# Neighbourhood attention: the context units spread in pairs over the four latent blocks, their outputs in the bank of the output transposes

## The chip, the cores and the metric

The kernel runs on one core of a Trainium2 chip. The metric is the device time of one launch in microseconds (us). TensorE is called PE below (PEld is its weight load), VectorE DVE, ScalarE ACT, GpSimd POOL and SyncE SP.

## The reference

One inference step of a two-layer trunk for 128 context tokens and 512 latent tokens with the same weights. Each layer has a mixer of three branches (differential attention, a state-space branch, neighbourhood attention) and a mixture of experts. Only the neighbourhood attention is touched. It has 8 heads of 64. Context tokens attend to all 128 context tokens:

```python
def block_attention(q, k, v):          # context: 8 heads, 128 queries, 128 keys
    ...
    s = jnp.einsum("bhqd,bhkd->bhqk", qi, k).astype(jnp.float32) * scale
    return jnp.einsum("bhqk,bhkd->bhqd", jax.nn.softmax(s, axis=-1).astype(v.dtype), v)

def neighbourhood_attention(q, k, v, kc, vc, rpb):   # latents, on a grid of 8 x 64
    ...                                # per block of 16 columns: 128 queries
        s_w = jnp.einsum("bhjqd,bhjkd->bhjqk", qi, kg).astype(jnp.float32) * scale + bi[None]
        s_x = jnp.einsum("bhjqd,bhcd->bhjqc", qi, kc).astype(jnp.float32) * scale
        pr = jax.nn.softmax(jnp.concatenate([s_w, s_x], axis=-1), axis=-1).astype(v.dtype)
        return (jnp.einsum("bhjqk,bhjkd->bhjqd", pr[..., :nk_blk], vg)
                + jnp.einsum("bhjqc,bhcd->bhjqd", pr[..., nk_blk:], vc))
```

A latent block has 256 window keys with a relative bias and a mask, and 128 cached context keys. The bias is added before the softmax.

## The kernel before

The program is written by hand for each engine, and semaphores alone order the engines against each other. `stage_na` runs once in each layer. It first projects v, q and k and gathers the values of each window into `vg`. Then comes the loop that the change touches.

**Units.** One unit is one block of 128 queries and one head. `units` lists them: block 0 (the context, 8 units), then blocks 1 to 4 of latents (8 each), 40 in all. Two units that follow each other are a pair, whose scores are computed together.

**What a unit does.** PE writes the scores into a bank of its own (banks 0 to 3 in turn; L1821 for the context, L1826 and L1829 for latents). DVE finds the maximum: for a context unit with one reduce from PSUM (L1950); for a latent unit it adds mask and raw bias (L1955), adds that to the scores and takes the maximum while it writes `pr` (L1960), and negates it (L1964). ACT takes the exponential into `pr` with the row sum (L1918 context, L1923 latent). PE transposes `pr` (`turn`, L1837: one transpose for the context, three for latents), ACT copies the result to `pT` (`evacuate`, L1910), and PE multiplies by the values into bank 6 (`values`, L1848 or L1853 and L1854). `pr` and `pT` have two buffers.

**The order on PE.** For pair g with the units 2g and 2g+1: scores of pair g+1, turn(2g), values(2g-1), turn(2g+1), values(2g). The order on ACT is exp(u), evacuate(u-1); on DVE it is maxima(u) in turn.

**The end of a block.** All eight heads of a block fill bank 6. After maxima of the second unit of the next block DVE waits for the last values of the block, forms reciprocals (L1969) and multiplies bank 6 into `o` (`take`, L1974). The first values of the next block wait for that, since they write the same bank. Two units on, PE transposes `o` in four pieces into bank 7 (`output`, L1863), and after the sixth unit's maxima DVE copies bank 7 in four pieces (L1988) to `oT` (`spill`), from which the next stage reads (PE L1269). After the last unit `take`, `output` and `spill` follow one another with nothing beside them.

**SP** issues the loads of the raw bias (L1734), four buffers ahead: load n waits for the mask addition of latent unit n-4.

## Time and profile before

| what | value |
|---|---|
| median of 3 runs | 2922.89 us (2920.81 to 2929.72) |
| the profiled execution | 2923.79 us, its span 2922.0 us |
| PE busy | 86% of the span |
| DVE, ACT, POOL busy | 32%, 20%, 13% |
| the loop over units, layer 0 | from 843.9 to 914.2 us of the span |
| the loop over units, layer 1 | from 2245.4 to 2313.8 us |

The two loops are 139 us of 2922. PE's granted clock is a share of 2.4 GHz: 1.00 is 2.4 GHz and 0.50 is 1.2 GHz.

### The profile page before, as it was taken

The page shows a single profiled execution, that of the slowest core. Times are in us where ns is not written, and L with a number is a line of the kernel's source. Part 1 is how long each engine was busy: PE and PEld are TensorE (multiplying, and loading weights), DVE is VectorE, ACT ScalarE, POOL GpSimd, SP SyncE. Part 2 cuts the span into 40 slices and gives each one's busy share as a digit, 9 for nine tenths or more (in the row PEclk, how much of TensorE's full clock was granted, in tenths as well). Part 3 has the DMA queues.
Part 4 walks back from the last instruction along what each step waited for, and adds up shares of the span by engine and source line. Part 5 has one row for each costly group of instructions (what it writes and reads, how often), then busy time and mean ns, then how long its engine had stood idle before and what let it go on. Part 6 is the DMA issues. An engine that isn't in the chain of part 4 may idle for free. (4 is left out here: it accounts for less than half of the span.)

```text
span 2922.0 us, 36075 instructions
## 1 busy us (share of the span) xinstructions
PE 2506.1 (86%) x13898; PEld 1488.6 (51%) x13898; DVE 944.7 (32%) x1843; ACT 598.7 (20%) x1392; POOL 366.8 (13%) x390
## 2 busy tenths in 40 slices
PE   5999999779999898868749998987999998988775
PEld 2445644556467546434325565545646764654442
DVE  1414311552026235111325242236301633522115
ACT  2221101430033021111142111024001401211111
POOL 0005100020002000222100250001200210022220
PEclk7999999899989998989969999989999999889997
DMA  8440053102631121788432102110033203075764
GB/s 311 145 149 33 29 201 134 37 1 80 201 99 32 63 94 70 281 334 312 170 129 96 37 29 75 36 58 1 29 129 96 43 29 119 29 269 226 279 235 180
DMA packets 170108, 357.95 MB, mean 123 GB/s; under 512 B 35076, under 2 KB 56684, under 8 KB 169972
## 3 DMA queue, kind: packets, MB, share of 16 engines
q1 hardware_dynamic: 129812, 267.70, 25.8%
q10 hardware_dynamic: 22176, 46.37, 4.6%
q0 software_dynamic: 17984, 42.01, 3.9%
q8 instruction: 92, 1.51, 0.2%
q14 instruction: 44, 0.36, 0.0%
HBM read 331.60 MB, written 47.48 MB: 130 GB/s over the span
## 5 line engine op out<-in xcount | busy, mean ns | idle before, releaser
L226 PE MATMUL ps<-hT,ring 128*128 128x512 f32 x896 | 413.4, 616 | 13.6 <-PEq L2822 12.4
L2297 PE MATMUL ps<-ring,mixT 128*32 128x256 f32 x2880 | 234.3, 407 | 73.4 <-issue 73.4
L226 PEld LDWEIGHTS ps<-hT,ring 128*128 128x128 f32 x896 | 172.8, 198 | 231.1 <-issue 230.8
L2297 PEld LDWEIGHTS ps<-ring,mixT 128*32 128x32 f32 x2880 | 124.5, 118 | 191.6 <-issue 129.1
L235 PE MATMUL ps<-ring,hT 128*128 128x512 f32 x480 | 211.8, 599 | 8.4 <-PEq L1182 7.4
L1220 POOL TENSOR_TENSOR mix_S<-ring 128x512 f32<-128x512 f32 x16 | 25.3, 1579 | 1160.7 <-POOLq L1357 607.4
L2181 PE MATMUL ps<-ring,mixT 128*128 128x512 f32 x320 | 143.9, 610 | 21.0 <-PEq L2822 21.0
L235 PEld LDWEIGHTS ps<-ring,hT 128*128 128x128 f32 x480 | 91.2, 192 | 122.1 <-issue 120.0
L1269 PE MATMUL ps<-late,ring 128*128 128x320 f32 x512 | 142.7, 436 | 5.6 <-PEq L1698 2.5
L2315 PE MATMUL ps<-ring,ex_hidT 128*32 128x512 f32 x800 | 117.1, 603 | 22.0 <-ACT ex_hidT L2404 22.0
L228 PEld LDWEIGHTS ps<-hT,ring 128*128 128x128 f32 x896 | 108.8, 192 | 26.8 <-issue 26.8
L1269 PEld LDWEIGHTS ps<-late,ring 128*128 128x128 f32 x512 | 96.9, 191 | 49.0 <-issue 9.5
L649 PE MATMUL ps<-hT,ring 128*128 128x512 f32 x256 | 112.8, 593 | 0.4 <-ACT ssm_dec L906 0.4
L2181 PEld LDWEIGHTS ps<-ring,mixT 128*128 128x128 f32 x320 | 62.1, 196 | 97.8 <-issue 97.8
L228 PE MATMUL ps<-hT,ring 128*128 128x128 f32 x896 | 109.1, 275 | 0.0
L1234 PE MATMUL ps<-mix_T,mix_S 128*128 128x320 f32 x384 | 106.0, 432 | 0.0
L2592 DVE TENSOR_TENSOR ex_hid<-ps,ex_silu 128x128 f32<-128x128 f32 x60 | 17.5, 291 | 271.4 <-ACT ex_silu L2399 271.4
L1234 PEld LDWEIGHTS ps<-mix_T,mix_S 128*128 128x128 f32 x384 | 73.0, 190 | 30.4
L2284 PE MATMUL ps<-base,mixT 128*128 128x128 f32 x496 | 68.6, 282 | 14.6 <-DMA mixT<-h_rows,ex_index 14.6
L649 PEld LDWEIGHTS ps<-hT,ring 128*128 128x128 f32 x256 | 48.4, 191 | 58.9 <-issue 58.8
L2609 DVE COPY out_gpost<-ps 128x512 f32<-128x512 f32 x60 | 41.5, 692 | 108.9 <-PE ps L2315 108.9
L2284 PEld LDWEIGHTS ps<-base,mixT 128*128 128x128 f32 x496 | 53.9, 142 | 40.1 <-issue 25.8
(439 smaller groups left out, 3904.2 us busy)
## 6 DMA issues: line engine op xcount, KB each, us to landing
ring<-in_w_in SPq DMA_DIRECT2D x18, 2048.0 KB, 9.1
ring<-in_w_gate SPq DMA_DIRECT2D x12, 2048.0 KB, 10.6
ring<-in_w_e_down SPq DMA_DIRECT2D x48, 512.0 KB, 11.9
ring<-in_w_e_gate SPq DMA_DIRECT2D x40, 512.0 KB, 7.7
ring<-in_w_e_up SPq DMA_DIRECT2D x40, 512.0 KB, 9.2
co_yg<-y_rows SPq DMA_DIRECT2D x40, 512.0 KB, 6.8
mixT<-in_w_ada ACTq DMA_DIRECT2D x8, 2048.0 KB, 8.7
da_ada_w<-in_w_ada ACTq DMA_DIRECT2D x8, 2048.0 KB, 8.9
```

The costliest lines, as they stand in the source:

```text
L226: pe.matmul(lat, wide[:, k, c], hT[:, k, CTX:TOK], start=(k == 0), stop=(k == kt_n - 1))
L228: last = pe.matmul(ctx, wide[:, k, c], hT[:, k, 0:CTX], start=(k == 0), stop=(k == kt_n - 1))
L235: last = pe.matmul(out, cx.hT[:, k, tok(t)], wide[:, k, :], start=(k == 0), stop=(k == KT - 1))
L649: ins = pe.matmul(ps[:, 6, :], wide[:, k, (m % 4) * P:(m % 4 + 1) * P], cx.hT[:, k, CTX:TOK], start=(k == 0), stop=(k == KT - 1))
L1220: pool.tensor_tensor(s1, a21, a22, ALU.add).then_inc(name("sums"), 1)
L1234: ins = pe.matmul(ps[:, bank(q, i), 0:HALF], left[:, k, :], right[:, k, :], start=(k == 0), stop=(k == KH - 1))
L1269: ins = pe.matmul(ps[:, BR + 2 * c + x, 0:HALF], wb[:, k, (2 * q + c) * P:(2 * q + c + 1) * P], cx.oT[:, k, half], start=(k == 0), stop=(k ...
L2181: ins = pe.matmul(ps[:, 2 * (t % 2) + n, :], cx.mixT[:, k, tok(t)], wide[n][:, k, :], start=(k == 0), stop=(k == KT - 1))
L2284: ins = pe.transpose(ps[:, k // 4, (k % 4) * P:(k % 4 + 1) * P], xg[:, b, k * P:(k + 1) * P], cx.ident)
L2297: ins = pe.matmul(ps[rows, 2 + b, 0:2 * P].rearrange("p (g f) -> p g f", g=2), xT[:, b, k, rows], ew[:, :, k, :], start=(k == 0), stop=(k ...
L2315: ins = pe.matmul(ps[rows, 4 + 2 * b + h, :], hidT[:, b, rows], slots[LANES * (s % 2) + c][1][:, h * SEC:(h + 1) * SEC], start=True, stop= ...
L2609: dve.tensor_copy(y[:, b, SEC:D], ps[:, 5 + 2 * b, :]).then_inc(sem("y_high"), 1)
```

## The change

The units get another order. Each latent block has four of its units, then two context units, then its other four: ten units in each of four rounds (`UPB`). The context's values go to the first 128 columns of bank 7, no longer to bank 6, and a small `take_ctx` on DVE brings each pair to `oc` (the free quarter of `vlo`), so that bank 6 holds latents alone. The values of the next context pair wait until bank 7 was spilled. The outputs come in the order of blocks 1, 2, 3, context, 4 (`taken`); that of the context stands just ahead of the last unit's values. Semaphore counts follow (`latents_to`). The diff, with the declarations of shapes left out:

```diff
--- before.py
+++ after.py
@@ -1694,7 +1694,17 @@
     KW = TOK + PAST
     ALLK = NKEY + PAST
 
-    units = [(b, h) for b in range(1 + NBLK) for h in range(NA_H)]
+    units = []
+    for b in range(1, 1 + NBLK):
+        units += [(b, h) for h in range(4)] + [(0, 2 * b - 2), (0, 2 * b - 1)] + [(b, h) for h in range(4, NA_H)]
+    UPB = NA_H + 2
+    latent = [unit for unit in units if unit[0]]
+    taken = list(range(1, NBLK)) + [0, NBLK]
+
+    def latents_to(u):
+
+        return sum(b > 0 for b, h in units[:u])
+
     with ExitStack() as st:
         def sb(name, shape):
             return st.enter_context(nc.sbuf_tensor(f"{name}_{L}", shape, F32))
...
@@ -1811,7 +1822,7 @@
                     if units[2 * g - 4][0] == 0:
                         pe.wait_ge(sem("na_exp"), 2 * g - 2)
                     else:
-                        pe.wait_ge(sem("na_s_read"), 2 * g - 2 - NA_H)
+                        pe.wait_ge(sem("na_s_read"), latents_to(2 * g - 2))
                 c = h // 2
                 q = [qT[64 * x:64 * x + 64, c, tok(b)] for x in range(2)]
                 k = [kT[64 * x:64 * x + 64, c, :] for x in range(2)]
@@ -1840,11 +1851,14 @@
             def values(u):
                 b, h = units[u]
                 pe.wait_ge(sem("na_pT_out"), u + 1)
-                if h == 0 and b >= 1:
-                    pe.wait_ge(sem("na_o_out"), b)
+                if h == 0 and b >= 2:
+                    pe.wait_ge(sem("na_o_out"), b - 1)
                 out = ps[:, 6, h * 64:(h + 1) * 64]
                 c = slice(h * 64, (h + 1) * 64)
                 if b == 0:
+                    if h >= 2 and h % 2 == 0:
+                        pe.wait_ge(sem("ona_out"), h // 2)
+                    out = ps[:, 7, (h % 2) * 64:(h % 2 + 1) * 64]
                     ins = pe.matmul(out, pT[:, u % 2, 0, :], v0[:, 0, c], start=True, stop=True)
                 else:
                     if b == 1 and h == 0:
@@ -1854,13 +1868,17 @@
                     ins = pe.matmul(out, pT[:, u % 2, 2, :], v0[:, 1, c], start=False, stop=True)
                 ins.then_inc(sem("na_o_mm"), 1)
 
-            def output(b):
-
-                pe.wait_ge(sem("na_o_out"), b + 1)
+            def output(n):
+
+                b = taken[n]
                 if b:
-                    pe.wait_ge(sem("ona_out"), b)
+                    pe.wait_ge(sem("na_o_out"), b)
+                pe.wait_ge(sem("na_c_out"), min(n + 1, NBLK))
+                if n:
+                    pe.wait_ge(sem("ona_out"), n)
+                src = o[:, (b - 1) % 2, :] if b else oc
                 for c in range(4):
-                    ins = pe.transpose(ps[:, 7, c * P:(c + 1) * P], o[:, b % 2, c * P:(c + 1) * P], cx.ident)
+                    ins = pe.transpose(ps[:, 7, c * P:(c + 1) * P], src[:, c * P:(c + 1) * P], cx.ident)
                 ins.then_inc(sem("ona_turned"), 1)
 
             ada.taken(pe, 4)
@@ -1872,8 +1890,9 @@
                 turn(u)
                 if u:
                     values(u - 1)
-                if u % NA_H == 2 and u > NA_H:
-                    output(u // NA_H - 1)
+                if u % UPB == 2 and u > UPB:
+                    output(u // UPB - 1)
+            output(NBLK - 1)
             values(len(units) - 1)
             output(NBLK)
 
@@ -1916,10 +1935,10 @@
                     act.wait_ge(sem("na_turned"), u - 1)
                 if b == 0:
                     act.activation(pr[:, u % 2, 0:CTX], ps[:, u % 4, 0:CTX], ACT.Exp, bias=nmx[:, u % 4:u % 4 + 1],
-                                   accum_out=sm[:, b % 2, h:h + 1]).then_inc(sem("na_exp"), 1)
+                                   accum_out=sm[:, 2, h:h + 1]).then_inc(sem("na_exp"), 1)
                 else:
-                    if h == 0 and b >= 2:
-                        act.wait_ge(sem("na_o_out"), b - 1)
+                    if h == 0 and b >= 3:
+                        act.wait_ge(sem("na_o_out"), b - 2)
                     act.activation(pr[:, u % 2, :], pr[:, u % 2, :], ACT.Exp, bias=nmx[:, u % 4:u % 4 + 1],
                                    accum_out=sm[:, b % 2, h:h + 1]).then_inc(sem("na_exp"), 1)
                 if u:
@@ -1950,7 +1969,7 @@
                     dve.tensor_reduce(nmx[:, u % 4:u % 4 + 1], ps[:, u % 4, 0:CTX], AX.X, ALU.max,
                                       negate=True).then_inc(sem("na_max"), 1)
                     return
-                n = u - NA_H
+                n = latents_to(u)
                 dve.wait_ge(sem(f"na_raw{n % 4}"), 16 * (n // 4 + 1))
                 dve.tensor_tensor(bias[:, u % 2, 0:NKEY], raw[:, n % 4, :], mask[:, b - 1, :], ALU.add).then_inc(
                     sem("na_bias_ready"), 1)
@@ -1964,20 +1983,34 @@
                 dve.tensor_scalar(nmx[:, u % 4:u % 4 + 1], mx[:, u % 4:u % 4 + 1], -1.0, None, ALU.mult).then_inc(
                     sem("na_max"), 1)
 
-            def take(b):
-
+            def take(b, u):
+
+                dve.wait_ge(sem("na_o_mm"), u)
+                dve.wait_ge(sem("na_exp"), u)
                 step(dve, dve.reciprocal(rc[:, b % 2, :], sm[:, b % 2, :]))
-                if b >= 2:
-                    dve.wait_ge(sem("ona_turned"), b - 1)
+                if b >= 3:
+                    dve.wait_ge(sem("ona_turned"), b - 2)
                 else:
                     dve.wait_ge(sem("na_v_dumped"), 64)
-                dve.tensor_tensor(o[:, b % 2, :].rearrange("p (h d) -> p h d", h=NA_H),
+                dve.tensor_tensor(o[:, (b - 1) % 2, :].rearrange("p (h d) -> p h d", h=NA_H),
                                   ps[:, 6, :].rearrange("p (h d) -> p h d", h=NA_H),
                                   spread(rc[:, b % 2, :], 2, NA_HD), ALU.mult).then_inc(sem("na_o_out"), 1)
 
-            def spill(b):
-
-                dve.wait_ge(sem("ona_turned"), b + 1)
+            def take_ctx(n, u):
+
+                pair = slice(2 * n, 2 * n + 2)
+                dve.wait_ge(sem("na_o_mm"), u)
+                dve.wait_ge(sem("na_exp"), u)
+                step(dve, dve.reciprocal(rc[:, 2, pair], sm[:, 2, pair]))
+                dve.wait_ge(sem("na_v_dumped"), 64)
+                dve.tensor_tensor(oc[:, n * P:(n + 1) * P].rearrange("p (x d) -> p x d", x=2),
+                                  ps[:, 7, 0:P].rearrange("p (x d) -> p x d", x=2), spread(rc[:, 2, pair], 2, NA_HD),
+                                  ALU.mult).then_inc(sem("na_c_out"), 1)
+
+            def spill(n):
+
+                b = taken[n]
+                dve.wait_ge(sem("ona_turned"), n + 1)
                 src = ps[:, 7, :].rearrange("p (c q) -> p c q", c=4)
                 for c in range(4):
                     if b == 0:
@@ -1990,15 +2023,14 @@
 
             for u, (b, h) in enumerate(units):
                 maxima(u)
-                if u >= NA_H and h == 1:
-                    dve.wait_ge(sem("na_o_mm"), b * NA_H)
-                    dve.wait_ge(sem("na_exp"), b * NA_H)
-                    take(b - 1)
-                if u >= NA_H and h == 5:
-                    spill(b - 1)
-            dve.wait_ge(sem("na_o_mm"), len(units))
-            dve.wait_ge(sem("na_exp"), len(units))
-            take(NBLK)
+                if u % UPB == 1 and u > UPB:
+                    take(u // UPB, UPB * (u // UPB))
+                if u % UPB == 5 and u > UPB:
+                    spill(u // UPB - 1)
+                if u % UPB == 8:
+                    take_ctx(u // UPB, u - 2)
+            spill(NBLK - 1)
+            take(NBLK, len(units))
             spill(NBLK)
 
 
```

The first place is PE's start of the loop in layer 0. The rows of before: context scores (L1821, two pairs), then transposes (L1837) and values (L1848) of one context unit each.

```order
L1821 MATMUL ps<-na_kT_0,na_qT_0 128x128 x4
L1837 MATMUL ps<-base,na_pr_0 128x128 x2
L1848 MATMUL ps<-na_v0_0,na_pT_0 128x64
L1821 MATMUL ps<-na_kT_0,na_qT_0 128x128 x2
L1837 MATMUL ps<-base,na_pr_0 128x128
L1848 MATMUL ps<-na_v0_0,na_pT_0 128x64
L1837 MATMUL ps<-base,na_pr_0 128x128
L1848 MATMUL ps<-na_v0_0,na_pT_0 128x64
```

The rows of the change at the same place, where L1837 and L1840 are the scores of a latent pair, L1848 the transposes, L1867 and L1868 the values of a latent unit, and L1832 the scores of a context pair:

```order
L1837 MATMUL ps<-na_kT_0,na_qT_0 128x256 x2
L1840 MATMUL ps<-na_kT_0,na_qT_0 128x128 x2
L1837 MATMUL ps<-na_kT_0,na_qT_0 128x256 x2
L1840 MATMUL ps<-na_kT_0,na_qT_0 128x128 x2
L1848 MATMUL ps<-base,na_pr_0 128x128 x6
L1867 MATMUL ps<-na_vg_0,na_pT_0 128x64 x2
L1868 MATMUL ps<-na_v0_0,na_pT_0 128x64
L1832 MATMUL ps<-na_kT_0,na_qT_0 128x128 x2
L1848 MATMUL ps<-base,na_pr_0 128x128 x3
L1867 MATMUL ps<-na_vg_0,na_pT_0 128x64 x2
L1868 MATMUL ps<-na_v0_0,na_pT_0 128x64
```

The first two score pairs are now latent ones, of two matmuls of 256 and two of 128 columns each, and the first context scores come after the values of one latent unit.

The second place is PE's rows around the first context pair (units 4 and 5) in the changed kernel; L1862 is the values of a context unit.

```order
L1837 MATMUL ps<-na_kT_0,na_qT_0 128x256 x2
L1840 MATMUL ps<-na_kT_0,na_qT_0 128x128 x2
L1848 MATMUL ps<-base,na_pr_0 128x128
L1867 MATMUL ps<-na_vg_0,na_pT_0 128x64 x2
L1868 MATMUL ps<-na_v0_0,na_pT_0 128x64
L1848 MATMUL ps<-base,na_pr_0 128x128
L1862 MATMUL ps<-na_v0_0,na_pT_0 128x64
L1837 MATMUL ps<-na_kT_0,na_qT_0 128x256 x2
L1840 MATMUL ps<-na_kT_0,na_qT_0 128x128 x2
L1848 MATMUL ps<-base,na_pr_0 128x128 x3
L1862 MATMUL ps<-na_v0_0,na_pT_0 128x64
```

Each of the context unit's transposes and values now stands between the transposes and values of latent units; before, all eight were ahead of the first of these.

The third place is PE's end of the loop. Before (L1863 is the output's transposes):

```order
L1837 MATMUL ps<-base,na_pr_0 128x128 x3
L1853 MATMUL ps<-na_vg_0,na_pT_0 128x64 x2
L1854 MATMUL ps<-na_v0_0,na_pT_0 128x64
L1853 MATMUL ps<-na_vg_0,na_pT_0 128x64 x2
L1854 MATMUL ps<-na_v0_0,na_pT_0 128x64
L1863 MATMUL ps<-base,na_vlo_0 128x128 x4
```

And in the changed kernel (L1881 the output's transposes):

```order
L1848 MATMUL ps<-base,na_pr_0 128x128 x3
L1867 MATMUL ps<-na_vg_0,na_pT_0 128x64 x2
L1868 MATMUL ps<-na_v0_0,na_pT_0 128x64
L1881 MATMUL ps<-base,na_vlo_0 128x128 x4
L1867 MATMUL ps<-na_vg_0,na_pT_0 128x64 x2
L1868 MATMUL ps<-na_v0_0,na_pT_0 128x64
L1881 MATMUL ps<-base,na_vlo_0 128x128 x4
```

The transposes of the context's output moved from the first latent block to this place, ahead of the last unit's values.

## Rows read from the trace of the kernel before

**Rows 1.** The page's first part, PE: busy, share, instructions; PEld and others follow.

```profile
PE 2506.1 (86%) x13898; PEld 1488.6 (51%) x13898; DVE 944.7 (32%) x1843; ACT 598.7 (20%) x1392; POOL 366.8 (13%) x390
```

**Rows 2.** Busy by stretch: length, PE, PEld, DVE, ACT, POOL, PEclk, DMA share, GB/s.

```profile
843.90:914.20 70.30, 64.40 (x477) 55.95 (x477) 45.37 (x167) 41.04 (x120) 0.03 (x1) 0.86 0.30 66
2245.40:2313.80 68.40, 62.22 (x477) 54.23 (x477) 45.39 (x167) 41.03 (x120) 0.04 (x1) 0.90 0.37 89
844.00:864.00 20.00, 19.05 (x89) 15.33 (x90) 8.67 (x31) 9.62 (x37) 0.00 (x0) 0.50 0.31 73
865.00:914.00 49.00, 44.27 (x381) 39.51 (x379) 36.46 (x135) 31.08 (x83) 0.00 (x0) 1.00 0.29 63
2245.40:2249.80 4.40, 3.56 (x26) 2.45 (x26) 1.37 (x6) 3.07 (x16) 0.00 (x0) 1.00 1.01 364
2250.00:2263.50 13.50, 13.07 (x62) 10.91 (x62) 7.21 (x25) 6.30 (x20) 0.00 (x0) 0.50 0.42 91
```

**Rows 3.** Timeline, PE, latent pairs at 2.4 GHz: start, busy, engine, line.

```profile
865.17 0.70 PE L1826 MATMUL ps<-na_kT,na_qT 64*128 64x256 f32 x4
...
866.02 0.55 PE L1837 MATMUL ps<-base,na_pr 128*128 128x128 f32 x3
...
868.07 0.70 PE L1826 MATMUL ps<-na_kT,na_qT 64*128 64x256 f32 x4
...
884.24 0.70 PE L1826 MATMUL ps<-na_kT,na_qT 64*128 64x256 f32 x4
...
888.15 0.70 PE L1826 MATMUL ps<-na_kT,na_qT 64*128 64x256 f32 x4
...
889.14 0.55 PE L1837 MATMUL ps<-base,na_pr 128*128 128x128 f32 x3
...
891.72 0.70 PE L1826 MATMUL ps<-na_kT,na_qT 64*128 64x256 f32 x4
```

**Rows 4.** Timeline, DVE, at 2.4 GHz, the last two after the end of a block.

```profile
869.02 0.43 DVE L1955 TENSOR_TENSOR na_bias<-na_raw,na_mask 128x256 f32<-128x256 f32 x1 [0.39 <-PE ps L1829]
...
887.14 0.42 DVE L1955 TENSOR_TENSOR na_bias<-na_raw,na_mask 128x256 f32<-128x256 f32 x1
...
888.30 0.42 DVE L1955 TENSOR_TENSOR na_bias<-na_raw,na_mask 128x256 f32<-128x256 f32 x1
```

**Rows 5.** Timeline, PE, a context pair at 2.4 GHz, layer 1.

```profile
2247.90 0.49 PE L1821 MATMUL ps<-na_kT,na_qT 64*128 64x128 f32 x4
2248.32 0.33 PE L1837 MATMUL ps<-base,na_pr 128*128 128x128 f32 x1
...
2249.38 0.49 PE L1821 MATMUL ps<-na_kT,na_qT 64*128 64x128 f32 x4
```

**Rows 6.** Timeline, PE and PEld, the start of the loop in layer 0.

```profile
843.93 1.23 PE L1821 MATMUL ps<-na_kT,na_qT 64*128 64x128 f32 x8 [4.54 <-ACT na_kT L1902]
...
851.50 1.23 PE L1826 MATMUL ps<-na_kT,na_qT 64*128 64x256 f32 x4
...
859.86 1.23 PE L1826 MATMUL ps<-na_kT,na_qT 64*128 64x256 f32 x4
...
861.44 0.90 PE L1837 MATMUL ps<-base,na_pr 128*128 128x128 f32 x3
...
863.09 0.87 PEld L1863 LDWEIGHTS ps<-base,na_vlo 128*128 128x128 f32 x4
```

**Rows 7.** Timeline, all engines, the end of the loop in layer 0.

```profile
904.99 0.70 PE L1826 MATMUL ps<-na_kT,na_qT 64*128 64x256 f32 x4
...
910.38 0.66 PE L1853 MATMUL ps<-na_vg,na_pT 128*128 128x64 f32 x4
...
911.30 0.20 DVE L1969 RECIPROCAL na_rc<-na_sm 128x8 f32<-128x8 f32 x1 [2.84 <-PE ps L1854]
...
912.98 0.88 DVE L1988 COPY late<-ps 128x128 f32<-128x128 f32 x4 [0.75 <-PE ps L1863]
...
914.19 6.16 PE L1269 MATMUL ps<-late,ring 128*128 128x320 f32 x22 [1.24 <-PEq L1698]
```

More of the change, by code:

```diff
@@ L1711, in stage_na @@
         o = vlo[:, 2:4, :]
+        oc = vlo[:, 1, :]
         stage = sb("na_stage", [P, NA_H, NA_HD])
@@ L1714, in stage_na @@
         nmx = sb("na_nmx", [P, 4])
-        sm = sb("na_sm", [P, 2, NA_H])
-        rc = sb("na_rc", [P, 2, NA_H])
+        sm = sb("na_sm", [P, 3, NA_H])
+        rc = sb("na_rc", [P, 3, NA_H])
         if L + 1 < DEPTH:
@@ L1729, in load_raw @@
             def load_raw(n):
-                b, h = units[NA_H + n]
+                b, h = latent[n]
                 at = h * RPB_ROW + RPB_FRONT + col0(b - 1) - QB_C * (b - 1)
```

## Prediction

> **What bounds the kernel now.** I read the page first, then the stretches, then the timeline of the loop. The page shows TensorE (PE) busy for 86% of the span and no other engine above 32% [rows 1]. The two loops over units take 70.3 and 68.4 us [rows 2], 138.7 of 2922, so 0.3% of the kernel (8.8 us, about what a measurement can tell from no change) is 6% of what the change touches.
>
> Inside the loop at 2.4 GHz PE is busy 44.3 of 49.0 us, DVE 36.5 and ACT 31.1 [rows 2]. A plain latent pair takes 2.90 us from scores to scores (865.17 to 868.07), of which the scores are 0.85 (to 866.02) [rows 3], and the two units 1.03 each. DVE needs 1.16 per unit (887.14 to 888.30) [rows 4], 2.32 per pair, so it isn't the limit: PE is. Where a block ends PE loses time: the pair whose second values wait for `take` lasts 3.91 (884.24 to 888.15), 1.01 more, and the next, which has the four transposes of `output` and an exponential that comes late, lasts 3.57 (to 891.72), 0.67 more [rows 3]. So a block takes 2 x 2.90 + 3.91 + 3.57 = 13.28 us.
>
> The other limit is PE's clock. It stood at 1.2 GHz from 844 to 864 in layer 0, and in layer 1 it was at 2.4 GHz to 2249.8 and at 1.2 from 2250 to 2263.5 [rows 2]. At 1.2 GHz the scores of a latent pair take 1.58 (859.86 to 861.44) and a unit's transposes and values 1.65 (861.44 to 863.09) [rows 6]: 4.88 a pair, so each microsecond of dense latent work at 1.2 GHz costs 1 - 2.90/4.88 = 0.41 us.
>
> **What the change removes and adds, all at 2.4 GHz first.** The matmuls, exponentials and maxima of all units are as many as before. I lay the new order out in slots, one for each pair, and add them up.
>
> The start. Before, the loop began with light context pairs; the first latent scores came 7.57 us in (843.93 to 851.50) [rows 6]. Now latents fill the pipeline. A bias addition starts 0.95 after its scores (868.07, 869.02) [rows 3, 4], and the transposes 2.00 after the bias addition (887.14, 889.14) [rows 3, 4]. So unit 0 is transposed at 2.95, unit 1 (1.16 later on DVE) at 4.1, and after ACT's copy the values of unit 0 end at about 5.1. Two pairs' scores (1.7) lie inside. First slot: 5.1; it can't be under 4.1 (unit 1), nor over the 6.3 that it takes at 1.2 GHz.
>
> A context pair among latents. At 2.4 GHz its scores take 0.42 (2247.90 to 2248.32) and the rest of its 1.48 (to 2249.38) is 1.06 for two units, with a wait in it [rows 5]. The slot of the context pair holds the next latent pair's scores (0.85), the values of the latent unit before (the larger part of 1.03, I take 0.62) and two context transposes and one context values (0.70 of that 1.06): 2.17. The slot ahead of it has context scores in place of latent ones: 0.43 less work, of which I keep 0.34, so 2.56. In blocks 2 to 4 that gain is zero, because there PE waits for the exponential anyway until 0.99 after the scores began (888.15, 889.14) [rows 3]: 3.57 stays. The slot behind it has 2.40 us of PE work, but PE has come there too early. DVE starts the bias of unit 6 at 0.95 of the context slot and that of unit 7 1.16 later, at 2.11; its transposes can start 2.00 after that, at 4.11; PE would be there at 2.17 + 1.30 = 3.47. It waits 0.64, and some 0.1 more for ACT's copy: 3.13, or 0.23 more than a plain pair. So each context pair costs 2.06 in block 1 and 2.40 in the others. **Bounds of this term:** below, nothing waits and it costs its PE work alone, 1.29 (0.42, and 1.06 less the wait of about 0.2); above, as much as a latent pair, 2.90. I take the chain since each of its links is a row.
>
> DVE gains four `take_ctx` per loop: a reciprocal and a 128x128 product, between nothing and 0.20 + 0.88/4 (the 128x8 reciprocal and one of the four copies of 128x128 [rows 7]), 0.42. In the slot behind the context pair DVE has fewer than 2.9 us of work in the 3.13, and four times in a loop the 0.42 lies there; if that cover were gone it would be 1.7 a loop. `spill` leaves its place between two latent maxima and lies where DVE has only two short context maxima; the wait of the next context values for it ends before PE comes there (about 7.5 against 9.3 us from the start of the block's `take` slot), so I cost it at nothing.
>
> Removed: one `take` stall (1.01) and one `output` slot (0.67), since only three block ends lie inside the loop now. They do not come back in full: the context's `output` and `spill` stand at the end. Before, DVE's last reciprocal started 0.92 after the last values (910.38, 911.30) [rows 7]. Now the context's four transposes come ahead of these values, and its copies (0.88 like those at 912.98 [rows 7]) keep DVE to about 911.83: 0.53 later.
>
> The sum of a loop at 2.4 GHz: block 1 is 5.1 + 2.56 + 2.17 + 3.13 + 2.90 = 15.86; blocks 2 and 3 are 3.91 + 3.57 + 2.17 + 3.13 + 2.90 = 15.68 each; block 4 is 3.91 + 3.57 + 2.17 = 9.65, then the last two pairs with the drain, 9.20 before (904.99 to 914.19 [rows 7]), plus 0.23 and 0.53. Together 66.8 us.
>
> **The clock.** Before, PE was busy 19.05 of 20.00 us at 1.2 GHz in layer 0 [rows 2], and the clock still rose only some 4 us after the third latent pair's scores (859.86 [rows 6], 864), that is in the first stretch in which latent transposes and values ran without a stop; the context units and the stall for the first `take` lay before. In the changed order the first such stretch is units 1 and 2, about 6 to 10 us into the loop. I take the rise there. Layer 0 then starts at 1.2 GHz (the 4.54 us idle before the loop [rows 6] stays), the fill takes 6.3 in place of 5.1, and 3.7 us of dense work cost 1.3 more: 66.8 + 2.5 = 69.3, against 70.3 before, 1.0 less. In layer 1 the fill leaves PE idle more than the context units did, so the clock falls as before some 4.4 us in; with some 3.5 us at 1.2 GHz it costs 1.4 (0.41 of each): 68.2 against 68.3 or 68.4, 0.1 less.
>
> The Trainium skill (TensorE: Matmul & The Clock Gate, Part 1) says that sustained matmul activity is what releases the slow clock. The 19.05 busy us at 1.2 GHz do not agree with that rule taken alone [rows 2]. By that rule the changed loop, dense with latents from its first microsecond, would be at 2.4 GHz in layer 0 before the fill is over, and the sum of that loop would be about 68.
>
> Sum: 1.0 + 0.1 = 1.1 us less. The profiled execution of before took 2923.79, 0.9 more than the median of 2922.89; less 1.1 that is 2922.7, and 2922 on the scale of the median.
>
> **The rivals.**
> The clock rises late (this one ends on the slower side). The stretch of units 1 and 2 is cut by the context pair right behind it, whose units are as light as those that ran at 1.2 GHz before. If it isn't enough, slots 2 to 4 run at 1.2 GHz too: context slot 3.9, the next 4.4, the fourth 4.88, together 13.2 against 8.2 at 2.4 GHz: 5.0 more per layer, so +4 in one layer and +9 with both, 2926 to 2932. For it: latents now run in the slow time that cheap context units used to fill, and these lost less there. It decides from the point that both layers are late.
>
> The context pairs cost only their PE work. Then each costs 1.29, not 2.06 to 2.40: 8.5 us less over both loops, 2913. For it speaks that DVE has 36.5 of 49 us [rows 2]; against it the chain from bias to transposes, 2.00 us in rows, that a short slot can't cover.
>
> The clock hardly falls. If layer 1 stays at 2.4 GHz and layer 0 rises within the fill, the loops take 66.8 and 68 (66.8 and the 1.2 by which the fill is longer): 3.9 less than before, 2919. Against it: with context units PE was busy 3.56 of 4.40 us [rows 2], and the clock fell.
>
> The raw bias comes late in layer 1. Load 4 is now issued some 7 us sooner, into DMA engines whose share was 1.01 in the first 4.4 us of that loop [rows 2] with a weight section and two stores. It is needed 9 us in. If it misses by what remains of that queue I estimate 2 us: 2924.
>
> **How the numbers follow.** My forecast has 0.50 (2922, by itself 2918 to 2926). Late clock: one layer 0.15, both 0.12. Context hidden 0.06. Clock hardly falls 0.10. Raw bias late 0.05, other 0.02. More than 0.3% slower is above 2931.7: late in both layers and the rest, 0.14. More than 0.3% faster is below 2914.1: context hidden, 0.06. Same: 0.80. The range is 2915 to 2933: it takes in the late clock in both layers and leaves out the hidden context.
>
> **What would show it.** Scores to scores in the changed trace: 2.2 for the context slot, 3.1 for the slot behind, with PE waiting for ACT's exponential of the block's fifth or sixth latent head; 3.91 still at three block ends, no longer at the first; the granted clock back at 1.00 about 854 us in layer 0 and 8 us into the loop in layer 1; the four context copies on DVE, some 0.5 us of them past the last values, ahead of the last reciprocal. The prediction is wrong if the clock stays at 0.50 past the second context pair, if PE waits for DVE's `spill` ahead of context values, or if a bias addition waits for a DMA.

## The result and the profile after

| | before | changed |
|---|---|---|
| median of 8 runs each | 2929.34 us (2916.45 to 2938.97) | 2942.20 us (2936.72 to 2949.04) |
| ratio, with its 95% interval | 1 | 1.0047 (1.0025 to 1.007) |
| the profiled execution, its span | 2923.79, 2922.0 us | 2936.91, 2935.1 us |
| loop over units, layer 0 | 70.3 us | 78.7 us |
| loop over units, layer 1 | 68.4 us | 71.1 us |

The changed kernel is 0.47% slower, where 0.04% faster was forecast, and its 2942.20 lies outside the range of 2915 to 2933. The kernel before took 6.4 us more here than the 2922.89 from which the forecast started; on that base 1.0047 would be 2936.6, outside the range as well. All ratios leave out three later executions (two of the kernel before, one with fills) of 5117 to 5254 us. Of the 13.1 us between the two spans, 11.1 lie in the two loops. The stages outside, whose code is the same, make up the other 2.0 (2785.3 us against 2783.3).

The page, its first part, changed kernel, against [rows 1]:

```profile
PE 2508.4 (85%) x13898; PEld 1489.8 (51%) x13898; DVE 946.5 (32%) x1855; ACT 597.5 (20%) x1392; POOL 366.5 (12%) x390
```

PE has as many instructions as before, and DVE twelve more. Nothing there tells of 13 us. The stretches do (length, PE, PEld, DVE, ACT, POOL, PEclk, DMA share, GB/s): first the two loops, then what lies inside them by granted clock, against [rows 2].

```profile
844.60:923.30 78.70, 70.12 (x477) 61.24 (x477) 46.35 (x173) 40.57 (x120) 0.04 (x1) 0.80 0.27 60
2258.60:2329.70 71.10, 61.03 (x476) 53.40 (x477) 46.35 (x172) 40.50 (x120) 0.00 (x0) 0.93 0.35 86
844.60:862.50 17.90, 16.82 (x82) 14.41 (x83) 7.62 (x28) 7.32 (x23) 0.00 (x0) 0.50 0.39 98
...
873.00:876.00 3.00, 3.00 (x16) 2.80 (x16) 0.88 (x4) 1.25 (x6) 0.00 (x0) 0.50 0.16 50
...
890.00:900.00 10.00, 10.00 (x51) 8.95 (x51) 4.36 (x17) 3.95 (x14) 0.00 (x0) 0.50 0.20 41
2258.60:2296.00 37.40, 31.81 (x270) 27.66 (x271) 26.62 (x98) 23.49 (x69) 0.00 (x0) 1.00 0.50 129
2296.50:2306.00 9.50, 9.50 (x48) 8.47 (x48) 3.88 (x14) 3.76 (x13) 0.00 (x0) 0.50 0.19 42
```

What to see: before, the clock rose once in each loop and stayed up to its end. Now it rises at 862.7, 18 us into layer 0, and then falls twice inside the latent blocks (about 872.7 to 876.2 and 889.8 to 900.1), and once in layer 1 (2296.1 to 2306.4). Read to 0.1 us, that is about 31.6 and 10.2 us at 1.2 GHz in the two loops, against 20.2 and 13.7 before. The forecast had about 10 and 3.5.

Layer 1 shows the new order at 2.4 GHz undisturbed for 37 us. Timeline of PE there (start, busy, engine, line; in brackets the idle time ahead and what ended it). L1837 is the scores of a latent pair, L1832 those of a context pair, L1848 transposes, L1867 values:

```profile
2258.60 0.70 PE L1837 MATMUL ps<-na_kT,na_qT 64*128 64x256 f32 x4 [0.83 <-ACT na_kT L1921]
...
2263.92 0.49 PE L1832 MATMUL ps<-na_kT,na_qT 64*128 64x128 f32 x4
...
2266.39 0.70 PE L1837 MATMUL ps<-na_kT,na_qT 64*128 64x256 f32 x4
...
2268.41 0.70 PE L1837 MATMUL ps<-na_kT,na_qT 64*128 64x256 f32 x4
...
2270.57 0.55 PE L1848 MATMUL ps<-base,na_pr 128*128 128x128 f32 x3 [0.45 <-ACT na_pr L1942]
...
2271.76 0.70 PE L1837 MATMUL ps<-na_kT,na_qT 64*128 64x256 f32 x4
...
2274.66 0.70 PE L1837 MATMUL ps<-na_kT,na_qT 64*128 64x256 f32 x4
...
2277.79 0.63 PE L1867 MATMUL ps<-na_vg,na_pT 128*128 128x64 f32 x4 [0.78 <-DVE na_vlo L1995]
...
2278.57 0.49 PE L1832 MATMUL ps<-na_kT,na_qT 64*128 64x128 f32 x4
2279.56 0.55 PE L1848 MATMUL ps<-base,na_pr 128*128 128x128 f32 x3 [0.50 <-ACT na_pr L1942]
...
2282.13 0.70 PE L1837 MATMUL ps<-na_kT,na_qT 64*128 64x256 f32 x4
...
2284.15 0.70 PE L1837 MATMUL ps<-na_kT,na_qT 64*128 64x256 f32 x4
...
2286.30 0.55 PE L1848 MATMUL ps<-base,na_pr 128*128 128x128 f32 x3 [0.49 <-ACT na_pr L1942]
...
2287.49 0.70 PE L1837 MATMUL ps<-na_kT,na_qT 64*128 64x256 f32 x4
...
2290.39 0.70 PE L1837 MATMUL ps<-na_kT,na_qT 64*128 64x256 f32 x4
```

From scores to scores, measured against forecast: fill 5.32 (5.1), context-score slot 2.47 (2.56), context slot 2.02 (2.17), the slot behind 3.35 (3.13), plain pair 2.90 (2.90). The next block: `take` 3.91 (3.91), `output` 3.56 (3.57), context 2.02 (2.17), behind 3.34 (3.13), plain 2.90. The first block is 16.06 against 15.86 and the second 15.73 against 15.68. So no slot is off by more than 0.22 us.

The same slots where the clock falls in the middle, layer 0, PE (L1881 is the transposes of `output`):

```profile
887.11 0.63 PE L1867 MATMUL ps<-na_vg,na_pT 128*128 128x64 f32 x4 [0.78 <-DVE na_vlo L1995]
...
887.89 0.49 PE L1832 MATMUL ps<-na_kT,na_qT 64*128 64x128 f32 x4
888.88 0.55 PE L1848 MATMUL ps<-base,na_pr 128*128 128x128 f32 x3 [0.50 <-ACT na_pr L1942]
...
890.02 1.06 PE L1881 MATMUL ps<-base,na_vlo 128*128 128x128 f32 x4
...
892.83 1.23 PE L1837 MATMUL ps<-na_kT,na_qT 64*128 64x256 f32 x4
...
896.53 1.23 PE L1837 MATMUL ps<-na_kT,na_qT 64*128 64x256 f32 x4
...
900.66 0.70 PE L1837 MATMUL ps<-na_kT,na_qT 64*128 64x256 f32 x4
```

The two waits (0.78 for `take`, 0.50 for an exponential) lie within 2.6 us, from 886.33 to 888.88. Behind them the `output` transposes take 1.06 in place of 0.61, and the slots 4.94, 3.70 and 4.13 in place of 3.56, 2.02 and 3.34. All three falls inside the blocks come at this point of a block, in its `output` slot.

In the old order the same place has one wait, not two. There the 0.78 for `take` stands as well, but the scores that follow are those of a latent pair; they last until 889.08 and the transposes start at 889.14 [rows 3], so the wait for the exponential is 0.06:

```profile
888.69 0.39 PE L1829 MATMUL ps<-na_kT,na_qT 64*128 64x128 f32 x4
```

The context scores are shorter, and leave 0.50 of it open.

### The profile page after: what moved, and what is told of

It reads as the page before. It is cut to its first block and busy times, and to the rows that moved or that the text cites. A ratio compares the mean times of both kernels' runs of the same rounds, so it can differ in the third digit from the quotient of the medians.

```text
span 2935.1 us, 36111 instructions
## 1 busy us (share of the span) xinstructions
PE 2508.4 (85%) x13898; PEld 1489.8 (51%) x13898; DVE 946.5 (32%) x1855; ACT 597.5 (20%) x1392; POOL 366.5 (12%) x390
## 5 line engine op out<-in xcount | busy, mean ns | idle before, releaser
L2329 PEld LDWEIGHTS ps<-ring,mixT 128*32 128x32 f32 x2880 | 124.6, 118 | 190.1 <-issue 127.7
L2316 PE MATMUL ps<-base,mixT 128*128 128x128 f32 x496 | 70.3, 286 | 16.2 <-DMA mixT<-h_rows,ex_index 16.0
L2316 PEld LDWEIGHTS ps<-base,mixT 128*128 128x128 f32 x496 | 55.2, 145 | 41.8 <-issue 27.3
```

The lines of the kernel that those rows point to most:

```text
L2316: ins = pe.transpose(ps[:, k // 4, (k % 4) * P:(k % 4 + 1) * P], xg[:, b, k * P:(k + 1) * P], cx.ident)
L2329: ins = pe.matmul(ps[rows, 2 + b, 0:2 * P].rearrange("p (g f) -> p g f", g=2), xT[:, b, k, rows], ew[:, :, k, :], start=(k == 0), stop=(k ...
```

## The experiments

My theory was that the falls come from the stretch between `take` and the end of the `output` slot, where three light places now stand together: the wait for `take`, the slot with context scores and its wait for an exponential, and the context slot. The rivals were that the new order is longer at any clock, that the low start is what costs, that the shared bank 7 costs something, and that the bias on DVE is the late link. Two remarks hold for all: single executions of one kernel differ by up to 1% here (the kernel before took 2915.80 to 2943.76 in 34 of them, and the same code outside the two loops took 2782.6 to 2796.2 us in the twelve traces), so that medians of 5 to 12 runs are compared with runs of the kernel before on the same chip; and matmuls called fills multiply values already in place into bank columns that nobody reads (those ahead of a loop into a bank that the scores overwrite), so that they change no result. Each run has one traced execution.

### The changed kernel again

No edit.

> The changed kernel once more, as a base for the others on the same chip. Both theories: 10 to 15 us over before. Theory C (clock): in each loop of the trace the granted clock falls to 0.50 again inside the blocks, right behind a take slot that is followed by a slot with context scores, and loop time is about 66.8 to 67.5 us plus 0.35 to 0.4 us for each microsecond at 0.50. Where the falls come may differ from one execution to the next. Theory D (dependencies alone): the loops take the same time whatever the clock does, and the extra lies in slots that are longer than before at the same clock.

Measured: 2945.96 us against 2927.69, 1.0063 (1.0043 to 1.0083). The loops took 78.50 and 74.64 us. Layer 0 again rose 18 us in, fell at 876.3, 28.0 us in, as far in as in the first trace (872.7 is 28.1 in), stayed down for 10 and fell once more at 910.4 for 3.4. Layer 1, which had not fallen at its start in the first trace, fell 5 us in here for 6.8, and again at 2320.5 for 10. All three falls inside blocks lie in `output` slots again. So a fall at a block's end recurs, while which blocks it hits differs from one execution to the next.

### Fills at the block ends

```diff
             def turn(u):
+                if u % UPB == 2 and u > UPB:
+                    pe.wait_ge(sem("na_pT_out"), u - 1)
+                    for _i in range(2):
+                        pe.matmul(ps[:, 4 + u % 2, 384:512], cx.ident, cx.hT[:, 0, 0:P], start=True, stop=True)
...
                 if h == 0 and b >= 2:
+                    for _i in range(3):
+                        pe.matmul(ps[:, 4 + u % 2, 384:512], cx.ident, cx.hT[:, 0, 0:P], start=True, stop=True)
```

> The changed kernel with matmuls of no use (results never read) where PE waits inside the blocks: three of 128x128 ahead of the wait for take, two ahead of the wait for the exponential one pair later, 0.24 us each at 2.4 GHz, in waits of 0.78 and 0.50 us. Theory C: more work for PE, yet the clock stays at 1.00 once it has risen, in both layers; the falls of 3.4, 10.3 and 10.2 us go, and the kernel is 7 to 10 us faster than the changed kernel. Theory D: the clock may stay up, but the time is the same or up to 2 us longer than that of the changed kernel, as each take slot stays at 3.91.

Measured: 2934.34 against 2927.69, 1.0028 (1.0009 to 1.0047), that is 11.6 us less than the changed kernel beside it (2945.96), with more for PE to do. Window from the rise to the end of the loop in layer 1:

```profile
2265.20:2322.80 57.60, 53.51 (x448) 47.06 (x446) 40.91 (x153) 35.29 (x104) 0.00 (x0) 1.00 0.27 56
```

After the low start each loop stayed at 2.4 GHz through all its block ends, for 57.6 us here and for 58 in layer 0. The loops took 71.52 and 70.33, 11.3 less than without fills. What follows: the falls inside the blocks hang on the waits at the block ends. By the medians the edit wins back 11.6 of the 18.3 us that the changed kernel lost on this chip. Not all of it need be those falls: in this trace the low start of layer 0 was 13.4 us long, not 18, though nothing was edited there.

### The context pair two units later

```diff
-        units += [(b, h) for h in range(4)] + [(0, 2 * b - 2), (0, 2 * b - 1)] + [(b, h) for h in range(4, NA_H)]
+        units += [(b, h) for h in range(6)] + [(0, 2 * b - 2), (0, 2 * b - 1)] + [(b, h) for h in range(6, NA_H)]
...
-                if u % UPB == 8:
-                    take_ctx(u // UPB, u - 2)
+                if u % UPB == 9:
+                    take_ctx(u // UPB, u - 1)
```

> The changed kernel with the context pair behind the sixth latent unit of each block, not the fourth, so that the slot with context scores is no longer the one with output's transposes. Theory C: PE's sparse slots stand apart, so the clock falls less often inside blocks: 5 to 10 us faster than the changed kernel. Theory D: the chain from bias to transposes is the same behind each context pair, so only the 0.34 us that the context scores save in a slot of their own comes back, three times a loop: about 2 us faster.

Measured: 2937.50 against 2927.69, 1.0038 (1.0022 to 1.0055), 8.5 us less than the changed kernel. The `output` slot now holds latent scores and is followed by a plain pair. Windows, layer 0, then layer 1:

```profile
855.00:908.50 53.50, 48.60 (x409) 42.45 (x408) 37.64 (x141) 34.72 (x107) 0.00 (x0) 1.00 0.27 59
2254.00:2270.50 16.50, 16.50 (x81) 14.62 (x81) 5.47 (x21) 7.02 (x23) 0.00 (x0) 0.50 0.39 92
2271.50:2318.50 47.00, 42.16 (x353) 36.81 (x353) 33.90 (x127) 30.31 (x91) 0.00 (x0) 1.00 0.27 57
```

Its PE rows at a block's end, layer 0:

```profile
866.13 0.63 PE L1867 MATMUL ps<-na_vg,na_pT 128*128 128x64 f32 x4 [0.65 <-DVE na_vlo L1995]
...
867.45 0.39 PE L1840 MATMUL ps<-na_kT,na_qT 64*128 64x128 f32 x4
867.90 0.55 PE L1848 MATMUL ps<-base,na_pr 128*128 128x128 f32 x3
```

No fall in the middle of a block is left. The loops were low at the start (in layer 0 down, up and down again in the first 10 us), and in the last 5 us of each; they took 69.66 and 75.05 us. The rows show why the block ends differ: the wait for `take` is still 0.65, but the latent scores run to 867.84 and the transposes start at 867.90, so the second wait is gone, as in the old order [rows 3], which stayed up too. So in these traces the `take` stall alone did not bring the clock down. Context scores in this place did, and they come with two things at once, less work for PE and a second wait of 0.50; which of them counts no run tells apart.

### The other bank alone, in the old order

```diff
-                if h == 0 and b >= 1:
+                if h == 0 and b >= 2:
                     pe.wait_ge(sem("na_o_out"), b)
-                out = ps[:, 6, h * 64:(h + 1) * 64]
+                out = ps[:, 6 if b else 7, h * 64:(h + 1) * 64]
```

(and the same bank in `take`).

> The order of before with one part of the change: the context's values go to bank 7, all eight heads, so that the first latent block's values need not wait for its take. Theory C and D alike: the first take stall goes (0.8 to 1.7 us a loop at 1.2 GHz), 2 to 3 us faster than before, within 0.3% of it. If the time rises by over 5 us, it is the bank, and not the order, that costs.

Measured: 2924.40 against 2927.69, 0.9994 (0.9978 to 1.0009), no difference. Its PE row at the first block end, layer 0:

```profile
858.56 0.55 PE L1837 MATMUL ps<-base,na_pr 128*128 128x128 f32 x3 [0.43 <-ACT na_pr L1923]
```

The wait for `take` is gone there, but the exponential is waited for. At 2.4 GHz the bank gains 0.13 us a loop, as the two experiments after this one show. So in the old order the bank costs nothing that can be measured. In the changed order bank 7 is also shared with the output transposes; there no context values (L1862) waited in either trace of the changed kernel.

### The old order with fills

```diff
+            for _i in range(4 if L == 0 else 1):
+                pe.matmul(ps[:, 3, :], cx.ident, cx.hT[:, 0, 0:512], start=True, stop=True)
             pe.wait_ge(sem("na_kc_out"), 1)
...
+                for _i in range(3 if u == 0 else 0):
+                    pe.matmul(ps[:, 4 + u % 2, 384:512], cx.ident, cx.hT[:, 0, 0:P], start=True, stop=True)
                 pe.wait_ge(sem("na_exp"), u + 1)
...
                 if h == 0 and b >= 1:
+                    for _i in range(3):
+                        pe.matmul(ps[:, 4 + u % 2, 384:512], cx.ident, cx.hT[:, 0, 0:P], start=True, stop=True)
                     pe.wait_ge(sem("na_o_out"), b)
```

(the wait for the exponential now stands behind that for `na_pT_out` and the fills).

> The order of before, with matmuls of no use (never read) where PE waits: four of 128x512 (layer 1: one) in the 4.5 us ahead of the loop, three of 128x128 ahead of the first exponential's wait and three ahead of each take's wait. It shows the old order at one clock. Theory C: the granted clock stays at 1.00 in most of both loops, each loop takes 64 to 65 us (70.3 and 68.3 before), and the kernel is 6 to 10 us faster than before. Theory D: the loops stay within 1 us of 70 and 68.

Measured: 2920.13 against 2926.41, 0.9974 (0.996 to 0.9989): faster than the kernel before, by 0.26%. Window of its loop in layer 0 (that of layer 1 is alike):

```profile
850.40:914.20 63.80, 59.66 (x506) 52.92 (x506) 45.35 (x166) 40.61 (x120) 0.00 (x0) 1.00 0.32 72
```

This is the number that my prediction lacked: the old order at 2.4 GHz from end to end takes 63.85 us a loop (63.87 and 63.83). The loops lost 10.9 us in the trace and the median 6.3. The interval of the ratio, 3.2 to 11.7 us, holds both, so nothing says that a part did not reach the end of the kernel.

### The same with the other bank

The two edits above together; with bank 7 the fills at block ends begin a block later.

```diff
-                if h == 0 and b >= 1:
+                if h == 0 and b >= 2:
+                    for _i in range(3):
+                        pe.matmul(ps[:, 4 + u % 2, 384:512], cx.ident, cx.hT[:, 0, 0:P], start=True, stop=True)
                     pe.wait_ge(sem("na_o_out"), b)
-                out = ps[:, 6, h * 64:(h + 1) * 64]
+                out = ps[:, 6 if b else 7, h * 64:(h + 1) * 64]
```

(and the same bank in `take`).

> The same fills, and the context's values in bank 7 for the order of before (no take stall for the first latent block). Theory C: loops of 63 to 64 us, 8 to 13 us faster than before in all. Theory D: only the first take stall goes, 2 to 3 us.

Measured: 2921.13 against 2926.41, 0.9974 (0.9956 to 0.9992). Loops of 63.74 and 63.71 us, 0.13 less each than with bank 6. In the run with this bank and no fills layer 1 took 63.58 us, at 2.4 GHz nearly throughout, so the fills themselves add next to nothing.

### The changed order with fills everywhere

The block-end fills of the second experiment, and those at the start:

```diff
+            for _i in range(4 if L == 0 else 1):
+                pe.matmul(ps[:, 3, :], cx.ident, cx.hT[:, 0, 0:512], start=True, stop=True)
             pe.wait_ge(sem("na_kc_out"), 1)
...
+                for _i in range({0: 4, 1: 2}.get(u, 2 if u % UPB == 2 and u > UPB else 0)):
+                    pe.matmul(ps[:, 4 + u % 2, 384:512], cx.ident, cx.hT[:, 0, 0:P], start=True, stop=True)
                 pe.wait_ge(sem("na_exp"), u + 1)
...
                 if h == 0 and b >= 2:
+                    for _i in range(3):
+                        pe.matmul(ps[:, 4 + u % 2, 384:512], cx.ident, cx.hT[:, 0, 0:P], start=True, stop=True)
```

> The changed kernel with fills of no use in all its waits: ahead of the loop, ahead of the exponentials of units 0 and 1, and the five per block end of the second run. With the clock at 1.00 throughout, what is left over the run with the old order and fills is the price of the order at one clock. Prediction from the slots: loops of 66.8 to 68 us, 3 us each over the old order with fills, because a context pair among latents costs 2.1 to 2.4 us and one among context pairs 1.48. Theory D's stronger form (the order costs all of it): 5 us or more over the old order in each loop. If the clock were all, the two kernels would be equal.

Measured: 2923.60 against 2926.41, 0.9981 (0.9966 to 0.9996). Windows of its two loops:

```profile
846.30:913.40 67.10, 61.36 (x518) 54.45 (x519) 46.26 (x172) 40.45 (x120) 0.01 (x1) 1.00 0.31 69
2248.90:2316.00 67.10, 61.34 (x518) 54.47 (x518) 46.30 (x172) 40.47 (x120) 0.00 (x0) 0.99 0.36 91
```

Narrowly read they are 67.14 and 67.23. The fills do not lengthen them: the second block of layer 1 takes 15.72 us here (2264.88 to 2280.60), 15.73 without fills. Two things follow. My sum at 2.4 GHz, 66.8, was right to 0.4 us. And the changed order needs 3.3 to 3.4 us a loop more than the old one at the same clock. This is read from the traces; the medians of the two kernels with fills, 2923.60 and 2920.13, differ the same way, but the intervals of their ratios overlap.

### The bias ahead of the scores

```diff
             def maxima(u):
-                dve.wait_ge(sem("na_scores"), u + 1)
-                if u >= 4:
-                    dve.wait_ge(sem("na_exp"), u - 3)
...
                 dve.tensor_tensor(bias[:, u % 2, 0:NKEY], raw[:, n % 4, :], mask[:, b - 1, :], ALU.add).then_inc(
                     sem("na_bias_ready"), 1)
+                dve.wait_ge(sem("na_scores"), u + 1)
+                if u >= 4:
+                    dve.wait_ge(sem("na_exp"), u - 3)
```

(a context unit keeps its waits in front).

> The changed kernel with one edit on DVE: a latent unit's mask addition, which doesn't need the scores, stands ahead of the wait for them, so that the chain from scores to transposes is up to 0.45 us shorter. If the wait behind each context pair comes from that chain, its 0.45 us idle on PE goes or shrinks below 0.2, and the slot there falls from 3.3 to about 3.0: 2 to 3 us in both loops, more if the clock falls less often. If the wait comes from ACT or bank 7, the slot stays at 3.3.

Measured: 2948.36 against 2926.41, 1.0076 (1.005 to 1.0103), not better than the changed kernel, 1.0047 and 1.0063. Its DVE rows behind a context pair, layer 1, at 2.4 GHz:

```profile
2310.60 0.56 DVE L1982 CUSTOM_DVE_ANT_0 na_pr<-ps,na_bias 128x384 f32<-128x384 f32 x1 [0.98 <-PE ps L1848]
...
2311.27 0.41 DVE L1974 TENSOR_TENSOR na_bias<-na_raw,na_mask 128x256 f32<-128x256 f32 x1
2311.93 0.56 DVE L1982 CUSTOM_DVE_ANT_0 na_pr<-ps,na_bias 128x384 f32<-128x384 f32 x1 [0.24 <-DVE na_bias L1974]
```

The first latent unit had its bias ready, but its place in `pr` came free only when PE had transposed the context unit that used it. And each unit now idles 0.24 us between its bias addition and the next step, where it was 0.03, so the units follow each other at 1.33 us (2310.60 to 2311.93) in place of 1.17. PE waited 0.61 behind the context pair, where it was 0.49, and 0.70 in the `output` slot, where it was 0.50. So the early bias opened one link and lengthened another, and the theory that the bias was the late link fell. The clock fell inside a block in both loops again (for 13.7 and 10.2 us), and they took 79.07 and 78.99 us.

### Fills at the start alone

The fills of the full version ahead of `na_kc_out` and for units 0 and 1, none at the block ends.

```diff
+                for _i in range({0: 4, 1: 2}.get(u, 0)):
```

> The changed kernel with the fills of no use at the start of the loop alone (ahead of it, and ahead of the exponentials of units 0 and 1), none at the block ends. It splits the clock's part in two. Theory C: the start is at 2.4 GHz in both layers (some 18 us at 1.2 GHz less in layer 0), but the clock still falls inside blocks, behind a take slot with a context slot after it, in one or both layers; loops of 67.2 us plus 0.35 to 0.4 per microsecond at 0.50; the kernel between the one with all fills and the changed one, 4 to 8 us faster than the changed kernel. If it stays up inside the blocks too, the falls there came from the low start and not from the block ends.

Measured: 2934.02 against 2923.64, 1.0043 (1.0028 to 1.0058). Windows, layer 0, then layer 1:

```profile
846.30:883.00 36.70, 32.29 (x277) 28.41 (x277) 26.04 (x95) 22.98 (x68) 0.00 (x0) 1.00 0.41 90
883.50:886.50 3.00, 3.00 (x17) 3.00 (x16) 0.98 (x5) 1.39 (x6) 0.00 (x0) 0.50 0.34 66
...
2250.60:2272.30 21.70, 18.95 (x162) 16.67 (x163) 15.07 (x56) 13.20 (x39) 0.00 (x0) 1.00 0.61 171
2273.00:2283.00 10.00, 10.00 (x51) 8.95 (x52) 4.17 (x16) 3.78 (x13) 0.00 (x0) 0.52 0.20 40
```

Each loop began at 2.4 GHz and fell all the same at block ends, twice in layer 0 and once in layer 1. So the falls don't need a low start. All three lie in `output` slots, as do all eleven falls inside blocks in the four traces with this order and no fills there (the two of the changed kernel, the early bias and this one). The loops took 70.34 and 71.52, in sum as much as with fills at the block ends alone (141.9 both), so in these two traces start and block ends cost about the same. The ratio, 1.0043, is not clear of the changed kernel's first 1.0047; the 4 to 8 us expected over the changed kernel are not shown by it, and this chip has no run of that kernel.

### One fill in place of two and three

```diff
-                    for _i in range(2):
+                    for _i in range(1):
...
-                    for _i in range(3):
+                    for _i in range(1):
```

> The second run's kernel (changed, fills at the block ends) with fewer of them: one 128x128 matmul ahead of the take's wait in place of three, one ahead of the exponential's wait in place of two. Theory C with a graded effect: part of the falls inside the blocks return, so the kernel lies between that with five and the changed one, 2936 to 2944. If a single one in each wait is enough, it equals the kernel with five fills, and the block ends lay only just under what keeps the clock up.

Measured: 2939.97 against 2923.64, 1.0052 (1.0036 to 1.0068), inside the 2936 to 2944 expected. Windows, layer 0, then layer 1:

```profile
862.60:917.50 54.90, 49.02 (x405) 42.74 (x404) 38.40 (x145) 33.01 (x98) 0.00 (x0) 1.00 0.25 54
2254.90:2291.80 36.90, 36.90 (x178) 32.86 (x178) 15.10 (x56) 15.23 (x47) 0.00 (x0) 0.50 0.29 62
```

Layer 0 kept its clock through the block ends. Layer 1 fell 5 us in, as in most executions, and did not rise again for 37.5 us, past two block ends, so that this loop took 82.03 us. No block end brought a fall here, and the slow time is all from the starts. The ratio lies between that with five fills (1.0028) and those with none (1.0047, 1.0063), and its interval overlaps with all three, so it doesn't say whether one fill is enough. The run leaves open, too, what holds the clock down once it is down.

## Why the prediction was wrong

**The sum at 2.4 GHz** was right: 66.8 against 67.14 and 67.23, with no slot off by more than 0.22 us. **The chain behind a context pair** was right in kind and, for the biases, in its rows. DVE, changed kernel, layer 1:

```profile
2267.39 0.43 DVE L1974 TENSOR_TENSOR na_bias<-na_raw,na_mask 128x256 f32<-128x256 f32 x1 [2.46 <-PE ps L1840]
...
2268.56 0.43 DVE L1974 TENSOR_TENSOR na_bias<-na_raw,na_mask 128x256 f32<-128x256 f32 x1
...
2286.60 0.17 DVE L2004 RECIPROCAL na_rc<-na_sm 128x2 f32<-128x2 f32 x1
2286.80 0.29 DVE L2006 TENSOR_TENSOR na_vlo<-ps,na_rc 128x128 f32<-128x128 f32 x1
```

The second bias starts 2.17 into the slot (2.11 forecast) and its transposes 2.01 later (2.00). PE came to that wait at 3.73, not 3.47, and so waited 0.45 us in place of 0.64: the slot is 0.2 longer than forecast because PE has more to do in it than I took. **`take_ctx`** takes 0.46 (0.42 forecast) and PE waits for none of it. **The end of the loop** too: PE, then DVE, layer 0.

```profile
918.97 0.61 PE L1881 MATMUL ps<-base,na_vlo 128*128 128x128 f32 x4
919.41 0.56 PE L1867 MATMUL ps<-na_vg,na_pT 128*128 128x64 f32 x4
...
919.61 0.89 DVE L2021 COPY late<-ps 128x128 f32<-128x128 f32 x4 [2.54 <-PE ps L1881]
...
920.41 0.19 DVE L1990 RECIPROCAL na_rc<-na_sm 128x8 f32<-128x8 f32 x1
```

The context's transposes push the last values back by 0.44, and the reciprocal starts 1.00 after these values where it was 0.92: 0.52 for the end, 0.53 forecast.

**The step that failed is the clock**, in the words of the prediction: "In the changed order the first such stretch is units 1 and 2, about 6 to 10 us into the loop. I take the rise there", and for layer 1 "with some 3.5 us at 1.2 GHz". In layer 0 it rose 18 us in (for good 10 to 18 us in, in the six traces with this start). In layer 1 the fall some 5 us in did come in five of the six traces with this start (not in that of the result itself) but lasted 7 to 37.5 us. Above all I let the clock rise once and stay. That it falls again inside blocks, at their `output` slots, stood in no case of mine, and in no sign of being wrong that I named. What that did to the sum can be read slot by slot. In layer 0 the first block took 22.05 us, 6.0 more than at 2.4 GHz, where I had added 2.5; the two falls cost 1.6 and 3.9. In layer 1 the fall cost 3.9, where I had 1.4 for a slow start that did not come. Of the 12.3 us by which the two loops exceed my 69.3 and 68.2, the falls inside the blocks are 9.3. That they come from the block ends is shown by pairs: with fills there they are gone (2.4 GHz for 57.6 us), with the context pair moved away they are gone, and with fills at the start alone they stay.

The size follows from the traces. In the changed loops 41.8 us at 1.2 GHz cost 149.8 - 134.4 = 15.4 us, 0.37 for each; in the old ones 33.9 cost 138.6 - 127.7 = 10.9, 0.32 for each (0.41 forecast). So of the 11.2 us (by narrow reading) that the loops grew, 4.5 are clock and 6.7 the order itself. In the second trace of the changed kernel the loops grew 14.5, of which 7.8 are clock: the order's part is fixed, the clock's differs between executions.

**The order's own price was in my rows, and I did not take it out.** I compared 66.8 with 70.3 and 68.4, which hold the slow time. By my own 0.41 the old loops' 33.5 us at 1.2 GHz cost 13.7, so the old order at 2.4 GHz was (138.7 - 13.7)/2 = 62.5 (63.85 measured). The change then had to win back 4.3 us a loop from the clock alone to break even, and the forecast stood on the weakest of its numbers. The cause of the price: a context pair among latents costs 2.02 + 3.34 - 2.90 = 2.46, among its own 1.48 [rows 5], 3.9 for four (0.4 less, as the slot with context scores in the first block took 2.47 and not 2.90); a block end fewer gives 1.7 of it back. The longer end (0.5) and, by subtraction, some 1.0 at the start make up the 3.3 that the runs show.

**The rivals.** The late clock came nearest: right sign, right engine, and right for the start of layer 0, where the context slot and the next took 3.70 and 3.88 (3.9 and 4.4 forecast; the clock rose inside the second). But it knew no falls later on, and so ended at 2926 to 2932. The 68 us for layer 0 that the prediction set beside its own sum did not come: PE was busy 16.82 of 17.90 us there at 1.2 GHz. The hidden context pair was wrong (2.46, not 1.29; its 8.5 us should also read 8.2 by its own costs). The clock that hardly falls was wrong. The raw bias was never late: every idle time ahead of a bias addition of the two loops ended with scores of PE, none with a DMA. The early-bias run also shows that the first link of my chain, that the bias waits for its scores, was not the one to shorten: behind it stands the free place in `pr`.

The Trainium skill (TensorE: Matmul & The Clock Gate, Part 1, on a second way in which the clock gate fails) tells of a kernel in which PE idles for moments between groups of matmuls, often enough that its clock swings between the two levels. The trace agrees that short waits suffice: no wait of PE in the middle of the loops is longer than 0.78 us, and the clock falls behind two of them, 0.78 and 0.50. The same part says that where the clock rises varies from run to run. The repeats of the changed kernel agree for the falls as well (there is one 5 us into layer 1 in one trace, and none there in the other).

**The best version** of those that ran is the old order with fills, 0.9974 (0.996 to 0.9989), with or without bank 7. It lies inside the 0.3% that I named as what a measurement can tell; with ten runs its interval leaves out 1 all the same.

## What to carry over

Before two orders are compared, take the slow-clock time out of both: sum the slots of the old order at 2.4 GHz as well as those of the new, and let the clock be a term of its own in each. Light work set beside a short stall can cost more than its own time where TensorE is the bound: it may open a second wait that heavier work had covered, and here the clock then fell for the heavy work behind it. Ask of every stall that is left what stands next to it, all through the loop and not at its start alone. A few matmuls of no use put into the waits are a cheap test of how much a kernel loses to its clock, and may be kept if they win.

## What the runs showed of the hardware

The granted clock stayed at 1.2 GHz with PE busy all the time: 10.00 of 10.00 us in the changed kernel, 36.90 of 36.90 in the run with one fill. And it stayed at 2.4 GHz with PE busy 31.81 of 37.40. So the busy share of the moment does not tell the level. In the old order with the other bank and no fills, layer 1 once ran at 2.4 GHz nearly to its end, with the same waits at its start as in the kernel before (0.83 and 0.69 us here, 0.83 and 0.68 there):

```profile
2248.20:2310.80 62.60, 56.71 (x476) 49.34 (x476) 44.79 (x164) 40.60 (x120) 0.00 (x0) 1.00 0.40 97
```

The two traces of the changed kernel, whose code is the same, differ in the same way. So the rise and fall depend in part on something that differs between executions. What it is I did not find out. With it, and with the spread of the stages outside the loops, effects of 0.3% needed medians of ten or so runs. On DVE, two waits put between a bias addition and the step that reads it left 0.24 us of idle time in each unit, where it had been 0.03.
